# Regrouping TensorE's small matmuls by sequence in the sample attention of a two-layer decoder

## What is computed

```python
def attn_mixer_sample(xn, kv_pool, kidx_pool, bufs, page_table, w_in, w_out, ...):
    ...
    # sparse heads: 8 query heads on 2 key heads, the keys picked by an indexer
    kv_sel = jnp.where((idx < past)[..., None, None, None], kv_past, kv_cur)
    o_a = sparse_attend(q_a, kv_sel[:, :, :, 0], kv_sel[:, :, :, 1], dist >= 0, dist, rel_bias[:, :A_HEADS])
    # three window groups of 4 heads: (window, dilation) = (128, 1), (512, 4), (2048, 16)
    for g, (win, dil) in enumerate(B_GROUPS):
        buf = bufs[g].astype(k_b.dtype)
        kv_all = jnp.concatenate([buf, jnp.stack([k_b[:, :, g], v_b[:, :, g]], axis=2)], axis=1)
        o, l = dilated_attend(q_b[:, :, g], kv_all[:, :, 0], kv_all[:, :, 1], wl + jnp.arange(t, dtype=jnp.int32),
                              dil, win // dil + 1, group_bias(rel_bias, g))
        outs.append(o)
        lses.append(l)
    o_b = merge_groups(outs, lses).astype(o_a.dtype)
    y = jnp.einsum('bte,ed->btd', jnp.concatenate([o_a, o_b], axis=-1), w_out)
```

## Time and profile before

| | before |
|---|---|
| median of 3 runs | 2963.74 us |
| the profiled execution's own time | 2963.74 us |
| its span, first to last instruction | 2961.9 us |
| TensorE busy in the span | 2694.1 us (91%) |
| mean granted TensorE clock | 0.944 |
| matmuls of the ten items | 846.57 to 875.9 us, about 29 us |
| merge, first matmul | 894.6 us |

### The profile page before, as it was taken

One profiled execution on the slowest core, in us unless ns is written; L12 is line 12 of the kernel. 1 busy time (PEld: TensorE's weight loads), 2 busy tenths in 40 slices (PEclk: granted clock), 3 DMA queues, 4 the chain that ended last, 5 costly groups with the idle time before them and its releaser, 6 DMA issues. The chain is left out here.

```text
span 2961.9 us, 39704 instructions
## 1 busy us (share of the span) xinstructions
PE 2694.1 (91%) x15960; PEld 2494.0 (84%) x15960; DVE 1250.0 (42%) x2228; ACT 644.7 (22%) x1148; POOL 949.9 (32%) x466
## 2 busy tenths in 40 slices
PE   6789998767863899999999998996999999999999
PEld 6557877754643899999999998886989999999999
DVE  5147888774625522222222235656342222222222
ACT  4242221644531211000100022345220110001100
POOL 3013440003703533234332344232332433333323
PEclk8889999867986999999999999998999999999999
DMA  4122222523144111111111111123111111111112
GB/s 137 70 57 64 88 80 84 178 58 109 46 128 164 50 43 43 42 42 43 48 43 44 42 43 60 63 81 142 51 38 43 43 42 42 46 46 42 42 42 82
DMA packets 109908, 196.49 MB, mean 66 GB/s; under 512 B 24205, under 2 KB 66317, under 8 KB 109517
## 3 DMA queue, kind: packets, MB, share of 16 engines
q1 hardware_dynamic: 109794, 194.97, 20.5%
HBM read 169.92 MB, written 46.06 MB: 73 GB/s over the span
## 5 line engine op out<-in xcount | busy, mean ns | idle before, releaser
L1992 POOL TENSOR_TENSOR unit_low<-unit_raw,unit_high 128x1024 fp32r<-128x1024 f32 x160 | 449.8, 2812 | 1238.9 <-DVE unit_high L1988 1238.3
L2284 DVE TENSOR_TENSOR x_t<-x_t,m_ps 128x1092 f32<-128x1092 f32 x128 | 165.4, 1293 | 523.3 <-PE m_ps L2005 523.3
L2005 PE MATMUL m_ps<-m_hidden_high,unit_high 128*128 128x364 f32 x1536 | 341.4, 330 | 2.9 <-POOL m_hidden_low L2191 2.7
L2005 PE MATMUL m_ps<-xg_high,unit_high 128*128 128x364 f32 x1536 | 339.8, 329 | 0.0
L2005 PE MATMUL m_ps<-m_hidden_high,unit_low 128*128 128x364 f32 x1536 | 339.7, 329 | 0.0
L2005 PE MATMUL m_ps<-m_hidden_low,unit_high 128*128 128x364 f32 x1536 | 338.9, 328 | 0.0
L2005 PE MATMUL m_ps<-xg_low,unit_high 128*128 128x364 f32 x1536 | 338.8, 328 | 0.0
L2005 PE MATMUL m_ps<-xg_high,unit_low 128*128 128x364 f32 x1536 | 338.0, 328 | 0.0
L2218 ACT ACTIVATE m_relu<-m_ps 128x1092 f32<-128x1092 f32 x64 | 69.4, 1084 | 1211.0 <-PE m_ps L2005 1211.0
L2272 DVE TENSOR_TENSOR m_relu<-m_relu,rstd_all 128x1092 f32<-128x1092 f32 x64 | 82.9, 1296 | 583.8 <-ACT m_relu L2218 583.8
L2005 PEld LDWEIGHTS m_ps<-m_hidden_high,unit_high 128*128 128x128 f32 x1536 | 265.5, 188 | 11.9 <-POOL m_hidden_low L2191 7.7
(11 more groups left out here) (332 smaller groups left out, 3822.4 us busy)
## 6 DMA issues: line engine op xcount, KB each, us to landing
unit_raw<-w_units SPq DMA_DIRECT2D x160, 512.0 KB, 3.5
w_raw<-w_in SPq DMA_DIRECT2D x48, 256.0 KB, 2.9
proj_rows<-rows SPq DMA_DIRECT2D x32, 256.0 KB, 2.0
s_win<-win_cache SPq DMA_DIRECT2D x2, 3968.0 KB
sw_rows<-proj_rows SPq DMA_DIRECT2D x16, 384.0 KB, 3.6
proj_rows<-rows SPq DMA_DIRECT2D x36, 128.0 KB, 1.8
select_work<-xt SPq DMA_DIRECT2D x8, 546.0 KB, 3.7
x_t<-xt SPq DMA_DIRECT2D x4, 1092.0 KB, 11.3
```

The lines of the kernel that those rows point to most:

```text
L1992: self.nc.gpsimd.tensor_tensor(self.wl[slot][:, :], self.raw[:, slot, :], self.wh[slot][:, :].bitcast(F32), ALU.subtract).then_inc(self.w_ ...
L2005: last = self.nc.tensor.matmul(ps[:, c, 0:CH], w[wslot][:, wk], v[:, k, c, :], start=(k == 0 and n == 0), stop=(k == nk - 1 and n == 2))
L2284: nc.vector.tensor_tensor(d.x[:, n, :, :], d.x[:, n, :, :], ps[s][:, :, 0:CH], ALU.add).then_inc(d.taken[s], 1)
```

## The change

In `scores` and in `outputs` the loops are swapped: the loop over the sequences (`bb`) becomes the outer one, and all matmuls of one sequence follow each other: both pages and the new keys in kind "a", both head pairs over old keys and both over new keys in kind "b", the old keys' values and then the new keys' values in the outputs. Number, shapes, operands and destinations of the matmuls stay the same, and so do all waits and signals. The other engines' programs do not change.

```diff
--- before.py
+++ after.py
@@ -1646,29 +1646,23 @@
                     pe.wait_ge(maxed, t - 1)
                 z = pss[t % 2]
                 if kind == "a":
-                    for n in range(NPAGE):
-                        for bb in range(2):
-                            b = 2 * i + bb
-                            nc.tensor.matmul(z[64 * bb:64 * (bb + 1), PAGE * n:PAGE * (n + 1)], qba[:, b, :],
-                                             kpa[:, NPAGE * b + n, :], start=True, stop=True)
                     for bb in range(2):
                         b = 2 * i + bb
-                        last = nc.tensor.matmul(z[64 * bb:64 * (bb + 1), w:w + DT], qba[:, b, :], kna[:, DT * b:DT * (b + 1)],
-                                                start=True, stop=True)
+                        o = z[64 * bb:64 * (bb + 1), :]
+                        for n in range(NPAGE):
+                            nc.tensor.matmul(o[:, PAGE * n:PAGE * (n + 1)], qba[:, b, :], kpa[:, NPAGE * b + n, :], start=True, stop=True)
+                        last = nc.tensor.matmul(o[:, w:w + DT], qba[:, b, :], kna[:, DT * b:DT * (b + 1)], start=True, stop=True)
                 else:
                     x = t - NA
                     pe.wait_ge(win_in[x], 16 * 5)
-                    for pair in range(2):
-                        for bb in range(4):
-                            b = 4 * i + bb
-                            nc.tensor.matmul(z[32 * bb:32 * (bb + 1), 0:w], qbb[:, g, pair, b, :],
-                                             kb[x][:, bb, w * pair:w * (pair + 1)],
+                    for bb in range(4):
+                        b = 4 * i + bb
+                        o = z[32 * bb:32 * (bb + 1), :]
+                        for pair in range(2):
+                            nc.tensor.matmul(o[:, 0:w], qbb[:, g, pair, b, :], kb[x][:, bb, w * pair:w * (pair + 1)],
                                              start=(pair == 0), stop=(pair == 1), tile_position=(0, 32 * bb))
-                    for pair in range(2):
-                        for bb in range(4):
-                            b = 4 * i + bb
-                            last = nc.tensor.matmul(z[32 * bb:32 * (bb + 1), w:w + DT], qbb[:, g, pair, b, :],
-                                                    knb[:, g, pair, DT * b:DT * (b + 1)],
+                        for pair in range(2):
+                            last = nc.tensor.matmul(o[:, w:w + DT], qbb[:, g, pair, b, :], knb[:, g, pair, DT * b:DT * (b + 1)],
                                                     start=(pair == 0), stop=(pair == 1), tile_position=(0, 32 * bb))
                 last.then_inc(scored, 1)
 
@@ -1690,16 +1684,17 @@
                 if t == NA:
                     pe.wait_ge(new_in, 16 * NG)
                 m, nb, ow = (64, 2, P) if kind == "a" else (32, 4, BW)
-                for n in range(w // P):
-                    for bb in range(nb):
-                        val = vpa[:, NPAGE * (nb * i + bb) + n, :] if kind == "a" else vb[t - NA][:, bb, n, :]
-                        nc.tensor.matmul(pso[t % 2][m * bb:m * (bb + 1), 0:ow], pt[:, t % 2, P * n + m * bb:P * n + m * (bb + 1)],
-                                         val, start=(n == 0), stop=False, tile_position=(0, m * bb))
                 for bb in range(nb):
                     b = nb * i + bb
+                    o = pso[t % 2][m * bb:m * (bb + 1), 0:ow]
+                    for n in range(w // P):
+                        val = vpa[:, NPAGE * b + n, :] if kind == "a" else \
+                            vb[t - NA][:, bb, n, :]
+                        nc.tensor.matmul(o, pt[:, t % 2, P * n + m * bb:P * n + m * (bb + 1)], val, start=(n == 0), stop=False,
+                                         tile_position=(0, m * bb))
                     val = vna[:, b, :] if kind == "a" else vnb[:, g, b, :]
-                    last = nc.tensor.matmul(pso[t % 2][m * bb:m * (bb + 1), 0:ow], pt[0:DT, t % 2, w + m * bb:w + m * (bb + 1)],
-                                            val, start=False, stop=True, tile_position=(0, m * bb))
+                    last = nc.tensor.matmul(o, pt[0:DT, t % 2, w + m * bb:w + m * (bb + 1)], val, start=False, stop=True,
+                                            tile_position=(0, m * bb))
                 last.then_inc(pv_done, 1)
 
             for t in range(NI + 2):
```

## The result

The changed kernel takes 3001.23 us, the median of 4 runs (2998.73 to 3003.79), against 2963.22 us (2960.57 to 2967.85) before: 1.0136 times, with a 95% interval of 1.0121 to 1.0150. It is slower by 38 us.

A forecast was written before the change was run, and what follows sets the result against it. TensorE's matmuls were taken to bound the stage; at clock 0.50 scores, outputs and transposes add 99.0 us, less vanishing waits +97, on 2963.7 us: forecast 3061 us, range 3003 to 3073 (own case 3040 to 3073).

The forecast's parts named there:

- What bounds the stage: Samples' attention stage: TensorE's matmuls set the pace (busy 28.2 of 30.2 us), so its gain or loss counts in full.
- How passes overlap: Scores and outputs: a tile takes one running and about three waiting passes; what stands behind them is not seen yet.
- The rival at clock 1.00: Clock 1.00 for most of the stage: nearly +42 us, 3006 us; chance 0.20, mixed clock included.
- The change of rows empties the whole array: Outputs: each switch between 128-row and 8-row passes empties all columns, losing 0.09 to 0.14 us behind the last pass.
- The clock: Whole stage: TensorE's clock stays at 0.50, as with the input projection's single 64x64 tiles.
- the stretch of the earlier trace: Input projection, 64x64 tiles one at a time: clock fell from 1.00 and stayed at 0.50, TensorE busy 3.42 of 3.42 us.
- the sum at 0.50: Scores, outputs and transposes added up at clock 0.50: +99.0 us, less vanishing waits, leaving +97.
- The waits that vanish: TensorE's waits in the stage, 1.1 us, and about 0.5 of VectorE's 1.6 us store wait go when TensorE is late.

## Why the prediction was wrong

- What bounds the stage: right. TensorE's 41.6 us more became 39.2 in the span, and no other engine or DMA took a share.
- How passes overlap: right, to a few hundredths. The rival at clock 1.00 had the scores' sequences 0.89 and 0.49 us apart; they came 0.89 and 0.47 apart. The block sizes show the edge at three waiting passes.
- The change of rows empties the whole array: right. The rival had 1.53, 1.09 and 0.95 us for a sequence; measured were 1.52, 1.09 and 0.94. In the changed order the next sequence's columns are idle and its first pass still starts 0.30 us behind the last 8-row pass of the one before.
- The clock: wrong, and this is the step that failed. The prediction put it as "The new order is like this: 32 of 128 columns at a time", and from that took 0.50 for the whole stage. It also called the stretch of the earlier trace rows back to back, but that holds only for the time after the fall: in the 3.41 us before it TensorE was busy for 2.88, with waits for ScalarE in between. So the stretch differs from the changed stage in two things: its tiles have 64 rows, and it waits. For the fall both were needed: back to back a 64x64 tile kept 1.00, with waits it fell, and with the same waits a 128x32 tile kept 1.00. But the changed stage begins at 0.50, so for it the way up counts, and there the rows alone made the difference: 64x64 and 64x32 tiles stayed at 0.50 for 41 us without any wait, a 128x32 tile, as narrow as the latter, was at 1.00 after 3.2 us. That step alone is some 55 us of the forecast: the sum at 0.50 gave +97, the same sum at 1.00 +42, and the stage measured +41.6.
- What the low clock would have cost the changed stage stays a sum on paper; no run put the whole stage there. What is left open is also why a tile's rows decide: the runs show only that they do.
- The rival's 3006 us stood 2.6 us above the profiled execution's 3002.9, nearly all of it the 2.4 us by which the span grew less than the stage; the median is 1.7 us lower still, within the spread of the 4 runs.
- The waits that vanish: 0.3 us is left of 1.1, nearly as said.

The Trainium skill's page "TensorE: Matmul & The Clock Gate" is met by the runs in one place and not in another. Its Part 1 has a busy engine leave the low clock: the changed stage and the 128x32 tile did, the 64x64 and 64x32 tiles, never idle for 41 us, did not. Its Part 3 has matmuls start strictly in program order: the trace of the changed kernel contradicts it, where a pass of the next sequence starts at 857.79 us and three that stand ahead of it in the program start from 857.81 on.

## What to carry to other kernels

Where several small matmuls share the array by columns, the order in the program may be by tile or across tiles, as long as no tile gets more than four passes in a row (two float32 matmuls here) and the matmuls with another number of rows stand together in a group of their own. Here each change of rows emptied all columns, so its cost was everything that could have run beside it, not the 0.09 us behind the last pass. A stretch of the trace is a weak witness for the clock of another one while rows or waits differ; here this one step was worth more (55 us) than all the others together (42).

## What was not expected of the hardware

- In one execution each: a single tile of 128 rows and 32 columns kept the clock at 1.00 for 20.8 us and raised it from 0.50 in 3.2 us; a tile of 32 rows and 128 columns let it fall in some 6 us.
- Tiles of 64 rows kept a high clock when back to back (20.8 us), lost it with waits in between (after 3.4 us), and did not regain it (41 us at 0.50).
- Blocks of 4 passes to one tile cost 0.04 us in an item of 1.10, blocks of 6 cost 1.37, blocks of 8 cost 2.66.
- The unchanged stage left the low clock 6.5 to 14.8 us after its first pass in different executions, and took 29.0 to 29.5 us with the early rise and 31.6 to 31.7 with the late one.
